# In each step of a stick-breaking loop VectorE makes the attention terms before it copies the output of the unit three steps back out of its PSUM bank

## The reference, cut to what matters

```python
for blk in range(S // SB_BLOCK):
    q0 = blk * SB_BLOCK
    q1 = q0 + SB_BLOCK
    z = jnp.einsum('bhqd,bhkd->bhqk', q[:, :, q0:q1], k[:, :, :q1]) * scale
    mask = jnp.arange(q1)[None, :] < (q0 + jnp.arange(SB_BLOCK))[:, None]
    log_1mb = jnp.where(mask, jax.nn.log_sigmoid(-z), 0.0)
    after = lax.cumsum(log_1mb, axis=3, reverse=True) - log_1mb
    A = jnp.where(mask, jnp.exp(jax.nn.log_sigmoid(z) + after), 0.0)
    outs.append(jnp.einsum('bhqk,bhkd->bhqd', A, v[:, :, :q1]))
```

## Time and profile before

| what | value |
|---|---|
| median of 3 runs | 1999.81 us (1998.1 to 2000.5) |
| profiled execution, its own time | 1998.87 us |
| its span, first to last instruction | 1997.2 us |
| PE busy | 1951.2 us (98%) |
| DVE, ACT, POOL busy | 756.0, 778.8, 851.5 us |
| mean granted TensorE clock | 0.993 |

### The profile page before, as it was taken

The page is one execution under the profiler, slowest core; times in us unless marked ns, Lnnn a source line. Parts: engine busy times, 40 slices in busy tenths (PEclk is TensorE's granted clock), DMA queues, the critical chain, the costliest instruction groups (busy, mean ns, idle before and its releaser), DMA issues.

```text
span 1997.2 us, 25482 instructions
## 1 busy us (share of the span) xinstructions
PE 1951.2 (98%) x9208; PEld 1620.8 (81%) x9208; DVE 756.0 (38%) x1205; ACT 778.8 (39%) x1523; POOL 851.5 (43%) x654
## 2 busy tenths in 40 slices
PE   7999999999999999999999899999999999999988
PEld 6777888988887888888888787888887888888877
DVE  3411322440224232222337864312376646024643
ACT  5422443513424333333355333153456645333332
POOL 6413444415254445444354443344343354445452
PEclk9999999999999999999999999999999999999999
DMA  6422333313133323333232232233222242333231
GB/s 194 116 58 75 94 85 85 85 43 106 57 111 97 125 88 107 106 95 95 79 101 79 60 105 69 59 95 90 69 74 69 69 133 68 101 95 91 89 106 53
DMA packets 98954, 178.51 MB, mean 89 GB/s; under 512 B 10763, under 2 KB 16503, under 8 KB 98860
## 3 DMA queue, kind: packets, MB, share of 16 engines
q1 hardware_dynamic: 94292, 170.68, 29.3%
q10 hardware_dynamic: 4568, 6.56, 1.2%
HBM read 173.26 MB, written 3.93 MB: 89 GB/s over the span
## 4 chain that ended last, share of the span: by engine, by line
issue 47%; PE 28%; POOL 22%; DVE 1%; ACT 1%; POOLq 1%; ACTq 0%; DVEq 0%
POOL w_lo L586 22%; PE proj L1836 9%; PE proj L1837 9%; PE proj L1838 9%; ACT arena L898 1%; POOLq L590 0%; PE work L1930 0%; DVE x L1499 0%; POOLq L588 0%; PE work L1966 0%; DVE arena L1498 0%; DVE arena L1238 0%; DVE arena L1501 0%; DVE arena L1505 0%; ACT w_hi L611 0%
## 5 line engine op out<-in xcount | busy, mean ns | idle before, releaser
L586 POOL TENSOR_TENSOR w_lo<-w_raw,w_hi 128x512 fp32r<-128x512 f32 x632 | 846.0, 1357 | 1117.8 <-ACT w_hi L611 977.9
L1836 PE MATMUL proj<-act_hi,w_hi 128*128 128x512 f32 (+1 forms) x1312 | 498.2, 380 | 8.9 <-DVE arena L1543 6.1
L611 ACT CAST w_hi<-w_raw 128x512 fp32r<-128x512 f32 x536 | 313.3, 618 | 479.5 <-PE proj L1838 458.5
L1837 PE MATMUL proj<-act_lo,w_hi 128*128 128x512 f32 (+1 forms) x1312 | 492.6, 375 | 0.0
L1838 PE MATMUL proj<-act_hi,w_lo 128*128 128x512 f32 (+1 forms) x1312 | 492.4, 375 | 0.0
L1836 PE MATMUL proj<-w_hi,act_hi 128*128 128x512 f32 x800 | 322.3, 403 | 6.6 <-POOL w_lo L586 5.1
L1838 PE MATMUL proj<-w_hi,act_lo 128*128 128x512 f32 x800 | 313.5, 392 | 0.0
L1837 PE MATMUL proj<-w_lo,act_hi 128*128 128x512 f32 x800 | 313.3, 392 | 0.0
L1836 PEld LDWEIGHTS proj<-act_hi,w_hi 128*128 128x128 f32 x1312 | 248.9, 190 | 57.7 <-issue 9.2
L1838 PEld LDWEIGHTS proj<-act_hi,w_lo 128*128 128x128 f32 x1312 | 248.6, 189 | 44.7
L1837 PEld LDWEIGHTS proj<-act_lo,w_hi 128*128 128x128 f32 x1312 | 248.7, 190 | 43.7 <-issue 0.5
(11 more groups left out here) (313 smaller groups left out, 1805.6 us busy)
## 6 DMA issues: line engine op xcount, KB each, us to landing
w_raw<-in_w_in SPq DMA_DIRECT2D x154, 256.0 KB, 2.8
w_raw<-in_w_in_ab SPq DMA_DIRECT2D x146, 256.0 KB, 2.7
w_raw<-in_w_mlp SPq DMA_DIRECT2D x128, 256.0 KB, 2.8
w_raw<-in_w_in_c SPq DMA_DIRECT2D x64, 256.0 KB, 2.8
w_raw<-in_w_out_ab SPq DMA_DIRECT2D x32, 256.0 KB, 2.7
w_raw<-in_w_out_c SPq DMA_DIRECT2D x32, 256.0 KB, 2.9
w_raw<-in_w_o_gla SPq DMA_DIRECT2D x16, 256.0 KB, 2.9
w_raw<-in_w_out SPq DMA_DIRECT2D x16, 256.0 KB, 2.7
```

The source lines that it names most:

```text
L586: return pool.tensor_tensor(w_lo[:, slot, :], w_raw[:, slot, :], w_hi[:, slot, :].bitcast(F32), ALU.subtract)
L611: act.copy(w_hi[:, b % RING, :], w_raw[:, b % RING, :]).then_inc(hi_ready, 1)
L1836: pe.matmul(out_, a_hi, b_hi, start=first, stop=False)
L1837: pe.matmul(out_, a_hi, b_lo, start=False, stop=False)
```

## The change

In the loop of VectorE the two duties change places. No instruction is added, removed or altered, on VectorE or on any other engine.

```diff
             for i in range(SB_STEPS + 1):
+                if i < SB_UNITS:
+                    terms(i)
                 if i >= 3:
                     output(i - 3)
-                if i < SB_UNITS:
-                    terms(i)
                 for s, j in beside[i]:
                     if j < s.n - 1:
                         continue
```

## The result

The changed kernel takes 2049.46 us (median of 4 runs, 2046.44 to 2051.47), against 1999.53 us before (4 runs). The ratio is 1.0249 with a 95% interval of 1.0231 to 1.0267, so it is 49.9 us slower. The forecast was 2045 us, with a range of 2033 to 2054. The profiled execution took 2046.44 us, 47.6 us more than that of before.

What follows compares the result with a forecast made beforehand. The prediction took PE's own queue to bound the loop. It added 38.1 us of waits and 7 us of lower clock to 1998.9 us, giving 2044, and with 0.9 us to the median 2045 us, range 2033 to 2054.

Steps and rivals of the forecast that it cites:

- The bound: In the changed loop only PE's queue sets the time, busy 189.96 of 192.00 us; any idle time is added.
- The mechanism: Inside one loop step, PE's values product now waits for scores, ScalarE's operations, VectorE's terms and the copy behind them.
- The waits by kind of step: PE's wait at L2335, for eight kinds by keys and projection blocks: none to 3.95 us, summing to 38.1 us.
- The 3.95 us of step 7: PE's predicted wait at L2335 in a loop step with 512 keys and one projection block.
- Adding up: Each loop wait puts off the next scores and terms equally, so the waits of 29 steps sum to 38.1 us.
- The part that was to come back: Where PE waits for ScalarE's late L1092, two places, up to 2.0 us return; set off against longer waits there.
- the kind put at 0.83: Loop steps with 128 keys and one projection block: a PE wait of 0.83 us each, 2 such steps.
- The clock: PE's clock falls behind about half of nine loop waits of 2.3 to 3.95 us: 7 us, bounds 0 and 13.6.
- Full clock with waits alone: Rival: PE's loop waits come but its clock stays at full, 2038 us on the median; chance 0.22.
- A loop with the clock low for most of the time: Rival: PE's share of the new chain takes longer too, time over 2054 us; chance 0.06.
- Smaller waits: Rival: loop waits under the sum, as terms may run shorter; half gives 2019 us, below 2033 needs a third gone; chance 0.07.
- The faster case: Rival: VectorE takes up terms sooner, L1092 follows, PE's 2.0 us of waits at L2324 go: 1998 us; chance 0.02.

Runs made afterwards that it cites:

- run with filled waits: Changed kernel, with 3, 9, 12 or 15 useless PE matmuls ahead of the transposes in steps with one projection block: 2040.02 us, ratio 1.0205.
- Two-block and one-block steps apart: Kernel before, terms ahead of the copy only in steps with two projection blocks, 2005.22 us, or only in those with one, 2041.62 us.
- run with half-filled waits: Changed kernel, with 2, 4, 6 or 7 useless PE matmuls ahead of the transposes in steps with one projection block: 2041.93 us, ratio 1.0215.
- run on one-block steps: Kernel before, with terms ahead of the copy only in steps with one projection block: 2041.62 us, ratio 1.0215.

## Why the prediction was right, point by point

**The bound was read rightly.** PE has no slack in the loop: 114 matmuls more cost 24.5 us there, and nothing behind the loop took back any of the new idle time.

**The mechanism was right.** The product with the values waits for a copy that stands behind the terms. With the copies on ScalarE and the same order of terms the 50 us vanish; with the copy ahead of the scan all but 2.5 do.

**The waits by kind of step were right to 0.1 us in the case shown.** The 3.95 us of step 7 came out as 3.76 us of recorded idle time in a step that is 4.0 us longer. The working had 0.05 us from the end of the copy to the start of the product; it is 0.14, and the copy starts 0.08 us ahead of the recorded end of L1713, which nearly cancels it. The sum was 38.1 us. The run with filled waits, the nearest to waits without low clock, gave 40.8. The idle time in the list, 34.9, is less than either, because a step grows by more than the idle time recorded in it (4.0 against 3.76), and because matmuls at the lower clock shorten the waits that follow: step 23, behind a fall, waits 0.55 us, and 0.94 with the waits filled.

**Adding up was right.** Two-block and one-block steps apart cost 6.0 and 42.4 us, together 48.4. The part that was to come back where ScalarE is late by itself was put at up to 2.0 us and was 1.4. That it is made up for by longer waits was only argued. The trace of the kernel before bears it out: the working of the prediction, done for each of the 29 steps by its own rows and not by eight kinds, sums to 40.6 us and not 38.1. Step 20, of the kind put at 0.83, shows it, VectorE first and then PE:

```profile
1538.75 1.06 DVE L1713 TENSOR_TENSOR arena<-arena,before_neg 128x128 f32<-128x128 f32 x1
```

```profile
1538.34 0.83 PE L2335 MATMUL work<-arena 128*128 128x128 f32 x6
```

This gives 1538.75 + 1.06 + 0.33 - 1538.34 = 1.80 us, and the changed kernel waited 1.64. Steps 17, 22 and 30 are also 0.3 to 0.6 us above their kind. Most of the difference is in the one-block steps, 31.8 us for 29.6. The two-block steps come to 8.9 for 8.4, and their run gave 6.0: 1.4 came back, and step 31, 1.43 by its own rows, had no wait in that run.

**The clock was right in kind and, at the median, set too small.** The prediction bounded it by 0 and 13.6 us and took 7. Against the run with filled waits it was 9.4 us at the median and 6.2 in the profiled execution, so 7 lies inside the spread of the changed kernel's own runs. That it came this near is in part luck, since "about half" had no row behind it. Six of nine long waits brought a fall in the profiled execution, more than the half assumed, at 1.7 us each in most cases and not 2.1. The places of the falls mattered less than thought: step 10 with 2.9 us of idle time had none, step 25 with 2.2 had one. The rule of the Trainium skill, that emptying PSUM by VectorE does not break the warmth of the clock (page "TensorE: Matmul & The Clock Gate", section "Loop structure matters more than you think"), did not carry over to this loop. Its example has the next matmuls follow at once, and here they waited for the copy, up to 3.76 us, with the clock at the lower level behind six such waits. The median of 2049.5 us is 4.5 above the forecast, and both terms were short: 38.1 for 40.8 and 7 for 9.4.

**The rivals.** Full clock with waits alone, 2038 us, is the run with filled waits at 2040. A loop with the clock low for most of the time did not come: its mean was 0.95. Smaller waits did not come either: the scan of 512 keys took 2.26 us in step 7 of the changed kernel, 2.28 before, and its terms took as long from the scores as before. This case was also worded loosely: a third of the sum must go to come below 2033 only with the 7 us of low clock, and at full clock some 5 of the 38 us are enough. The faster case asked for VectorE's earlier start to reach ScalarE, and its 8.4 us less of waiting at the copy were matched by more waiting for the logarithm.

## What to carry to other kernels

When an engine has two duties in a step, one short that another engine waits for and one long that waits for fresh data, the short one belongs ahead, even if the engine then seems to wait more for its own inputs. Idle time of an engine with slack is no reason to reorder it: VectorE's 18.9 us of waits for PE cost nothing, and taking 8.4 of them away cost 50. The price of such a move can be read before it is made: for each kind of step, the end of the long duty plus the short one, less the moment at which the waiting engine comes by. Here, on a full TensorE, the clock came on top, 9.4 us on 40.8 at the median. It is better worked out step by step than by kinds of step, where the rows are there.

## What the runs showed of the hardware that was not expected

Idle stretches of about 2 us, of which the prediction had one case (2.0 us before L1836), brought TensorE's clock to the lower level again (2.02 and 2.24 us in the run with half-filled waits, 2.18 in step 25 of the changed kernel), while others of 2.2, 2.6 and 2.9 us in the changed kernel did not. The length of the wait does not settle it. Steps 17 and 22 of the run on one-block steps show this best:

```profile
1541.29 2.05 PE L2338 MATMUL work<-arena 128*128 128x128 f32 x8 [2.61 <-DVE arena L1718]
...
1580.45 0.46 PE L2338 MATMUL work<-arena 128*128 128x128 f32 x2 [3.20 <-DVE arena L1718]
```

In the 5 us behind them the mean granted clock was 0.67 after the wait of 2.61 us and 1.00 after that of 3.20. In the changed kernel it was the other way round in the same two steps, 1.00 after 2.61 us and 0.69 after 3.21. What decides is open. The four timings of the changed kernel go with this: 2046.4 and 2047.5 us at a mean granted clock of 0.989, 2051.4 and 2051.5 at 0.986, as if two or three more of the waits had brought a fall (an estimate from 1.7 us for each; no trace of those two runs was kept). With the waits filled the runs lie within 0.7 us of each other, and the work that fills them makes the kernel 9.4 us faster.
